# One dense slot of a gate projection issued ahead of the sums of squares that follow a chunked scan

## The reference, cut to what matters

```
proj = u @ w_in          # q_a k_a v_a z_a beta_a dec_a q_b k_b v_b gate_a gate_b
y_a = rmsnorm(chunk_delta_rule(q_a, k_a, v_a, ...), o_norm_w) * silu(z_a)
q_b = rmsnorm(q_b, q_norm_w);  k_b = rmsnorm(k_b, k_norm_w)     # per head of 128
y_b = softmax(q_b k_b^T * scale + rel_bias[bucket], causal) v_b
mix = sigmoid(gate_a) * (y_a @ w_branch_gdn) + sigmoid(gate_b) * (y_b @ w_branch_moba)
h = h + mix @ w_out
```

## Time and profile before

| | us |
|---|---|
| median of 3 runs | 3486.75 |
| lowest, highest | 3484.26, 3487.68 |
| the profiled execution | 3484.84 |
| its span | 3482.7 |
| PE busy in the span | 3284.2 (94%) |
| DVE busy | 1423.2 (41%) |
| ACT busy | 474.7 (14%) |
| mean granted clock of TensorE | 0.966 of full speed |

### The profile page before, as it was taken

How to read it: one execution, slowest core, us unless ns; L and a number is a source line. 1 busy time by engine, 2 the same in 40 slices (tenths; PEclk the granted TensorE clock), 3 DMA queues, 4 the chain that set the end, 5 groups by cost and what they waited for, 6 DMA issues and landing times.

```text
span 3482.7 us, 50175 instructions
## 1 busy us (share of the span) xinstructions
PE 3284.2 (94%) x20868; PEld 2906.3 (83%) x20868; DVE 1423.2 (41%) x2155; ACT 474.7 (14%) x799; POOL 127.1 (4%) x89
## 2 busy tenths in 40 slices
PE   5899998989999999988999999999898999999999
PEld 4777787868888877777888887688787999999999
DVE  5447624354130133312265741161104555555443
ACT  2114410000000122211130002211000000000000
POOL 0003310000000000001000000000000000000000
PEclk9999999999999999998999999999999999999999
DMA  9763466656464422233335342232532444444443
GB/s 410 296 255 145 172 265 242 273 212 275 178 269 169 145 97 96 96 121 120 107 136 181 145 157 97 97 129 91 187 138 104 169 169 169 169 169 163 165 167 132
DMA packets 50897, 598.55 MB, mean 172 GB/s; under 512 B 9511, under 2 KB 12086, under 8 KB 13278
## 3 DMA queue, kind: packets, MB, share of 16 engines
q1 hardware_dynamic: 50782, 596.88, 45.3%
HBM read 593.70 MB, written 3.16 MB: 171 GB/s over the span
## 4 chain that ended last, share of the span: by engine, by line
PE 81%; DMA 9%; DVE 6%; ACT 1%; issue 1%; DVEq 1%; SPq 1%; ACTq 0%; POOLq 0%; POOL 0%
PE bank L261 27%; PE bank L2020 23%; PE bank L284 13%; DMA ring<-in_t_mod 9%; PE bank L275 5%; PE bank L296 3%; DVE E L324 3%; PE bank L2034 1%; PE aux L1209 1%; PE bank L362 1%; PE aux L1164 1%; DVE arena L324 1%; PE aux L844 0%; PE aux L1198 0%; PE bank L862 0%
## 5 line engine op out<-in xcount | busy, mean ns | idle before, releaser
L261 PE MATMUL bank<-arena,ring 128*128 128x256 f32 x3072 | 685.3, 387 | 25.6 <-DVE arena L1938 10.0
L261 PEld LDWEIGHTS bank<-arena,ring 128*128 128x128 f32 x3072 | 595.6, 194 | 112.7 <-issue 28.3
L261 PE MATMUL bank<-hT,ring 128*128 128x256 f32 x2560 | 565.1, 384 | 4.2 <-DVE hT L608 4.2
L261 PEld LDWEIGHTS bank<-hT,ring 128*128 128x128 f32 x2560 | 492.8, 193 | 73.8 <-issue 5.4
L284 PE MATMUL bank<-hT,ring 128*128 128x256 f32 x2304 | 533.7, 384 | 0.0
L284 PEld LDWEIGHTS bank<-hT,ring 128*128 128x128 f32 x2304 | 430.7, 191 | 75.4 <-issue 20.6
L2020 PE MATMUL bank<-arena,ring 128*128 128x128 f32 x3440 | 396.4, 275 | 0.0
L2020 PEld LDWEIGHTS bank<-arena,ring 128*128 128x128 f32 x3440 | 390.2, 192 | 0.0
L2020 PE MATMUL bank<-hT,ring 128*128 128x128 f32 x1680 | 197.9, 275 | 0.0
L2020 PEld LDWEIGHTS bank<-hT,ring 128*128 128x128 f32 x1680 | 192.7, 192 | 0.1
L324 DVE SCALAR_TENSOR_TENSOR E<-ring,c_act,E 128x512 f32<-128x512 f32 x240 | 180.9, 754 | 18.5 <-issue 0.6
(11 more groups left out here) (385 smaller groups left out, 2893.8 us busy)
## 6 DMA issues: line engine op xcount, KB each, us to landing
ring<-in_t_mod SPq DMA_DIRECT2D x64, 2048.0 KB, 15.7
ring<-in_t_gu SPq DMA_DIRECT2D x44, 2048.0 KB, 7.9
ring<-in_t_out SPq DMA_DIRECT2D x16, 2048.0 KB, 7.8
ring<-in_t_zs SPq DMA_DIRECT2D x16, 2048.0 KB, 8.0
ring<-in_t_down SPq DMA_DIRECT2D x16, 2048.0 KB, 7.2
ring<-in_t_gdn SPq DMA_DIRECT2D x12, 2048.0 KB, 7.9
ring<-in_t_u SPq DMA_DIRECT2D x8, 2048.0 KB, 8.5
ring<-in_t_z SPq DMA_DIRECT2D x8, 2048.0 KB, 8.3
```

Source lines behind the costliest of these rows:

```text
L261: last = nc.tensor.matmul(bank[s][:, T * f:T * f + T], w[:, j, P * f:P * f + P], act[:, j, :], start=j == 0, stop=j == kd - 1)
```

## The change

The products of the first of `gb`'s four slots stand right behind `pe_scan` in PE's list. Those of the other three stand where all four stood. `dense_slot` (L268) is a function that the kernel already has; for a slot it issues the same waits, the same 32 products and the same signal as `dense` (L251), which was used before. The lists of ACT, DVE, POOL and SP are as they were.

```diff
             pe_scan(pe)
+            dense_slot(pe, "gb", 0, 0, hT)
             pe_head_squares(pe, 1, o_sq, 4)
             pe_head_squares(pe, 2, B(2), 8)
             pe_bias(pe)
-            dense(pe, "gb", hT)
+            for s in range(1, COUNT["gb"]):
+                dense_slot(pe, "gb", 0, s, hT)
             pe_moba(pe)
```

## The result

The changed kernel takes 3493.64 us (median of 18 runs, 3490.98 to 3495.77), the one before 3486.82 (18 runs, 3482.13 to 3489.53). The ratio is 1.0019, with a 95% interval of 1.0012 to 1.0026, which is 4.2 to 9.1 us. So it is slower by 6.8 us; 7.3 were forecast, and 3494.1 as the time. That the change is slower is clear of noise. On which side of 0.2% it lies is not: the interval has both, so the 0.52 that the prediction put on a loss of more than 0.2%, against 0.41 on less than that either way, is neither borne out nor refuted.

What follows compares the result with a forecast made beforehand. TensorE was taken to bound the kernel (81% of the chain of waits), with 2.91 us of slack for VectorE's chain. Late chain +4.4 and clock +2.9 gave +7.3 us, a median of 3494.1 us, range 3488.0 to 3498.0.

Steps and rivals of the forecast that it cites:

- The slot moves up at no cost of its own: First gb slot directly behind the scan: start cost of leaving the scan's loop taken as 0, bounds 0 to 2.9 us.
- PE's own path, 5.0 sooner: PE from the scan to the end of gb: free at 2320.4, 5.0 us earlier than 2325.41.
- The idle 2.9: PE's 2.9 us of idle time behind the scan, while ACT squares the scan's output, was to go.
- the 1.8 of slow clock: First eight records of squares behind the scan's idle time: the slow clock's cost of 1.8 us was to go.
- VectorE's chain, 7.2 later: VectorE from first reciprocal to second bias addition: starts 7.2 us later, at about 2268.45, and ends at 2329.7.
- Scores 4.4 later, idle 9.4: Scores on PE wait for VectorE's chain: start at 2329.8, 4.4 us later, behind 9.4 us of new PE idle time.
- The clock, 2.9: PE from the scores on, behind the new idle time: lowered clock costs 2.9 us.
- The bounds of 1.8 to 3.1: Range given for the clock's loss on PE behind 9.4 us of idle time: 1.8 to 3.1 us.
- SP and the loads of `gb2`, nothing: SP's four gb2 loads slide by 7.2 us, the first lands at 2332.2 and costs 0, bounds 0 to 6.0 us.

Runs made afterwards that it cites:

- short chain: Reciprocals of the first four of eight q_b and k_b roots left out, in both orders: changed order 3479.67 us (ratio 0.9981), old order 3485.63 us (1.0004).
- the slot between the sums: Against the kernel before, the first gb slot stands between the first four sums of squares and the other eight: 3485.00 us, ratio 1.0000.
- the kernel with two slots: Against the changed kernel, two gb slots instead of one stand ahead of all twelve sums of squares: 3506.05 us, ratio 1.0058 to the kernel before.
- the kernel with the filling: Changed kernel plus 21 unused products of 128x256 in PE's wait ahead of the scores: 3489.34 us, ratio 1.0012 to the kernel before.
- the kernel with seven products ahead: Against the kernel before, seven of the first gb slot's 32 products ahead of the squares, 25 between four sums and eight: 3481.57 us, ratio 0.9990.

## Why the prediction was right

- *The slot moves up at no cost of its own.* It begins 0.16 us behind the last scan group's start, and 64 records pass before the first sum, at 2268.77. Leaving the scan's loop cost nothing that shows.
- *PE's own path, 5.0 sooner.* The short chain laid it bare: 5.25 in the trace. The idle 2.9 went as stated. The 24 records of the squares with their gaps took 12.69 us before (2255.76 to 2268.45) and 10.45 now, 2.24 less: the 1.8 of slow clock and 0.4 of gaps.
- *VectorE's chain, 7.2 later.* Measured from the scan's end, the first reciprocal moved from 8.71 to 15.81, so 7.1. The sums moved further, 10.8 (14.03 against 3.23 behind the scan's last group). The chain was spared the difference because before the change its first root did not wait for PE but for ACT, with its second squaring (3.60 us) and a table load of 1.28; now ACT stands idle for 7.11 us and PE's sum ends that. The chain itself took 61.62 us (2270.55 to 2332.17) against 61.26, and the 0.36 more are the bias load (9.70 us of wait for it against 9.34). ACT's table load in the kernel before, which ends at 2260.51, just ahead of the first root at 2260.52:

```profile
2259.23 1.28 ACT L1466 ACT_TABLE_LOAD   x1
```

- *Scores 4.4 later, idle 9.4.* Measured 4.41 (77.51 less 73.10) and 9.49. That the 4.4 is hit to the hundredth is luck. The prediction held the new start of the first product, 2329.8, against the old start of its weight load, 2325.41; the old product started at 2325.63, so like for like its terms give 4.2, and the slack up to the product was 3.1, not 2.91. The chain's start 0.1 sooner than forecast and the bias load 0.36 longer make up the difference. The mechanism stands all the same. That the wait is VectorE's, and that its slack was the point from which it decides, is shown by the pair with the short chain and by the slot between the sums.
- *The clock, 2.9.* This term was too large by 0.7, and that is nearly all of the sum's error. The slow stretch lasts 4.45 us behind this wait, half of which is 2.2, and 5.05 behind the 22.6 us of the kernel with two slots, 2.5. I had taken the middle of three stretches from elsewhere in the program, whose losses are 2.6 to 3.1. The bounds of 1.8 to 3.1 held it. The Trainium skill, "TensorE: Matmul & The Clock Gate", Part 1, whose advice would have dropped the term, puts such a loss below 1% of a typical kernel's span. The trace agrees, as 2.2 of 3491.6 us are 0.06%. But they are a third of what this change costs, so the term had to stay.
- *SP and the loads of `gb2`, nothing.* In the changed kernel the first load, issued at 2320.71, lands 14.0 us later, at 2334.7, and is wanted at 2335.6. At full clock PE would want it 1.8 sooner, and in the kernel with the filling it is late by 0.4, so the slow clock covers it. The prediction had this too: 2332.2 for the landing, between the 2331.7 of the full clock and the 2333.6 of the half. The fourth load did come nearer, issued 0.5 us behind the third, but it did not slow the others. Load by load, the four took 14.0, 16.3, 20.7 and 25.0 us, against 13.6, 16.6, 21.0 and 13.2 in the kernel before. The first three kept their times, and the fourth, behind them in the queue, took the longer. The Trainium skill, "DMA: Bandwidth & Descriptors", section "Queues, rings and completion order", is in agreement with that.

The sum, from the trace: 4.4 for the scores, 2.2 for the clock, 6.6, where 7.3 was forecast.

## What to carry to other kernels

Filling an engine's idle time with later work pays only as far as the filling fits the hole. Whatever overhangs delays what stood there, and when that is the head of another engine's long chain, the chain's slack at its far end is the budget, here 2.9 us against a delay of 7.1. Read the slack where the two paths meet before moving anything, and cut the filling to the size of the hole: 3.0 us of products instead of 13.8, with the chain's head moved up, made the same idea a gain of 4.6 us in the trace instead of a loss of 6.6.

## What was not expected of the hardware

- A wait of 1.90 us left TensorE's clock at full speed (the kernel with seven products ahead), one of 2.89 halved it for part of the next 5.40, and one of 22.59 did little more than one of 9.49: 5.05 and 4.45 us at 1.2 GHz. Through the 2.89 us themselves the granted clock stood at 1.00, so it fell only when PE was at work again.
- The code up to the scan's end, the same in all kernels here, reached that end at times up to 5.6 us apart in ten profiled executions (2250.88 to 2256.46). I did not look into what moves it; it is as large as the effects studied here.
